# A block chain on Trainium2: the operands of the delta rule prepared without Pool, with r by channel tiles in front and the key products between the steps of the first inverse

## The reference, cut to what matters

```
kk = k * k_k;  kk = kk / max(|kk|, 1e-12)          # per head
k  = k * (1 + (a - 1) * k_a)
for t in tokens:                                    # state S is 64x64 per head
    S = S * w_t + (S @ (-kk_t)) (kk_t * a_t)^T + v_t k_t^T
    y_t = S @ r_t
y = group_norm(y) * lnx_g + lnx_b + sum(r * k * r_k) * v
out = x + gate * ([y * silu(g_r), y_a * silu(g_a)] @ w_out)
```

## Time and profile before

| | |
|---|---|
| median of 3 runs | 1930.52 us (1925.89 to 1934.94) |
| profiled execution | 1928.67 us, span 1926.8 us |
| TensorE busy | 1851.0 us, 96% of the span |
| VectorE busy | 1028.7 us, 53% |
| ScalarE busy | 648.9 us, 34% |
| Pool busy | 172.2 us, 9% |
| granted TensorE clock, mean | 0.983 |
| stretch of the second block's projections and delta rule | about 1430 to 1790 us |

### The profile page before, as it was taken

How to read it: one execution, slowest core, us unless ns; L and a number is a source line. 1 busy time by engine, 2 the same in 40 slices (tenths; PEclk the granted TensorE clock), 3 DMA queues, 4 the chain that set the end, 5 groups by cost and what they waited for, 6 DMA issues and landing times.

```text
span 1926.8 us, 27348 instructions
## 1 busy us (share of the span) xinstructions
PE 1851.0 (96%) x11475; PEld 1529.8 (79%) x11475; DVE 1028.7 (53%) x1440; ACT 648.9 (34%) x999; POOL 172.2 (9%) x190
## 2 busy tenths in 40 slices
PE   7999999999999999999999999999989899998978
PEld 7879868888888898889868888878867787776546
DVE  4467347444454564446336556654566655445653
ACT  4332442323334322232432332334346232333441
POOL 3101001000000010001001000000020211111330
PEclk9999999999999999999999999999999999999998
DMA  8323323333323324332333545423232211114111
GB/s 269 113 88 109 99 66 99 120 93 94 98 88 121 98 90 119 98 110 99 99 105 122 155 149 164 143 88 99 77 109 61 59 57 35 46 35 143 41 37 44
DMA packets 145257, 189.65 MB, mean 98 GB/s; under 512 B 7688, under 2 KB 94980, under 8 KB 144240
## 3 DMA queue, kind: packets, MB, share of 16 engines
q1 hardware_dynamic: 139088, 168.32, 28.0%
q0 software_dynamic: 3488, 10.07, 1.6%
q10 hardware_dynamic: 2560, 9.53, 1.3%
HBM read 181.58 MB, written 6.30 MB: 98 GB/s over the span
## 4 chain that ended last, share of the span: by engine, by line
PE 87%; DVE 6%; issue 2%; ACT 2%; DMA 1%; POOL 1%; POOLq 0%; ACTq 0%; DVEq 0%
PE ps L324 25%; PE ps L325 24%; PE ps L326 24%; PE ps L2039 2%; PE ps L932 1%; PE ps L908 1%; PE ps L2025 1%; DVE WL L308 1%; PE ps L1472 1%; PE ps L2000 1%; ACT WH L298 1%; DMA RAW<-ab_w_in 1%; PE ps L509 1%; PE ps L2160 1%; PE ps L1493 1%
## 5 line engine op out<-in xcount | busy, mean ns | idle before, releaser
L308 DVE TENSOR_TENSOR WL<-RAW,WH 128x1024 fp32r<-128x1024 f32 x289 | 356.6, 1247 | 526.2 <-ACT WH L298 525.5
L324 PE MATMUL ps<-XH,WH 128*128 128x512 f32 (+1 forms) x1416 | 525.5, 371 | 3.9 <-DVE XL L522 3.5
L326 PE MATMUL ps<-XH,WL 128*128 128x512 f32 (+1 forms) x1416 | 519.2, 367 | 0.0
L325 PE MATMUL ps<-XL,WH 128*128 128x512 f32 (+1 forms) x1416 | 519.2, 367 | 0.0
L298 ACT ACTIVATE WH<-RAW 128x1024 fp32r<-128x1024 f32 x289 | 301.6, 1057 | 609.8 <-PE ps L326 577.9
L324 PE MATMUL ps<-WH,XH 128*128 128x512 f32 x800 | 322.4, 403 | 11.8 <-issue 4.2
L325 PE MATMUL ps<-WL,XH 128*128 128x512 f32 x800 | 315.4, 394 | 0.0
L326 PE MATMUL ps<-WH,XL 128*128 128x512 f32 x800 | 314.9, 394 | 0.0
L324 PEld LDWEIGHTS ps<-XH,WH 128*128 128x128 f32 x1416 | 268.8, 190 | 55.5 <-issue 9.3
L326 PEld LDWEIGHTS ps<-XH,WL 128*128 128x128 f32 x1416 | 268.5, 190 | 43.8
L325 PEld LDWEIGHTS ps<-XL,WH 128*128 128x128 f32 x1416 | 268.9, 190 | 41.5 <-issue 0.5
(11 more groups left out here) (332 smaller groups left out, 1960.3 us busy)
## 6 DMA issues: line engine op xcount, KB each, us to landing
RAW<-ffn_w_up SPq DMA_DIRECT2D x176, 256.0 KB, 3.2
RAW<-ffn_w_down SPq DMA_DIRECT2D x44, 512.0 KB, 3.6
RAW<-w_in SPq DMA_DIRECT2D x33, 512.0 KB, 3.9
RAW<-xa_wkv SPq DMA_DIRECT2D x32, 512.0 KB, 4.0
RAW<-c_w_in SPq DMA_DIRECT2D x24, 512.0 KB, 3.7
LATE<-w_ada SPq DMA_DIRECT2D x24, 512.0 KB, 4.9
RAW<-xa_wq SPq DMA_DIRECT2D x16, 512.0 KB, 5.5
RAW<-xa_wo SPq DMA_DIRECT2D x16, 512.0 KB, 3.7
```

The lines of the kernel that those rows point to most:

```text
L308: e.tensor_tensor(wl[:, :, 0:w], raw(i)[:, :, 0:w], wh[:, :, 0:w].bitcast(F), ALU.subtract).then_inc(*w_lo.up(i))
L324: e.matmul(o, lh, rh, start=start, stop=False)
L325: e.matmul(o, lh, rl, start=False, stop=False)
L326: return e.matmul(o, ll, rh, start=False, stop=stop)
```

## The change

The preparation has ten turns in place of eleven, and Pool has no part in it any more. On VectorE b and a fall on one turn. r is made by channel tiles (`r_dve`): tiles 0 to 2 at turn 7, tile 3 at turn 9, with k, formerly Pool's, at turn 8 between them. kt, rk and the `rkb` columns move to `tail_dve`, steps 3, 5 and 7 of the first inverse; rk moves from Pool to VectorE. Waits follow: the products with kt wait for kt, the others for r.

```diff
--- before.py
+++ after.py
@@ -1401,8 +1401,7 @@
                 elif i:
                     e.wait_ge(*at_pe.at(("qk", 0, 3)))
                 else:
-                    e.wait_ge(*pr_v.at("r"))
-                    e.wait_ge(*pr_g.at("rk"))
+                    e.wait_ge(*pr_v.at("rk"))
                 e.wait_ge(*p2_a.at(("qkv", i, n)))
                 e.activation(sq[i][n % 2], QK[i][0][n], ACT.Square).then_inc(*at_a.up(("sq", i, n)))
             if n == 4:
@@ -1803,7 +1802,7 @@
             e.matmul(b[:, :], selT[:, 128 * m:128 * m + 128], rs8, start=True, stop=True).then_inc(*pr_pe.up(("norm", m)))
             ps.back(("norm", m))
         yield
-        for n in range(6):
+        for n in range(5):
             yield
 
     def prep_act(e):
@@ -1837,7 +1836,7 @@
         yield
         e.wait_ge(*pr_a.at("p"))
         e.activation(B[2], B[2], ACT.Exp, scale=-1.0).then_inc(*pr_a.up("1/p"))
-        for n in range(5):
+        for n in range(4):
             yield
 
     def prep_dve(e):
@@ -1866,7 +1865,6 @@
         e.wait_ge(*pr_a.at(("x0", 3)))
         e.wait_ge(*pr_v.at("kk"))
         e.scalar_tensor_tensor(out=B[1], in0=B[1], scalar=1.0, in1=L[3], op0=ALU.add, op1=ALU.mult).then_inc(*pr_v.up("b"))
-        yield
         e.wait_ge(*pr_a.at("p1"))
         e.wait_ge(*spx.at("x"))
         e.scalar_tensor_tensor(out=ar[:, :, 0, :], in0=L[3].rearrange(by_col, j=64), scalar=-1.0,
@@ -1876,33 +1874,23 @@
         e.wait_ge(*pr_v.at("b"))
         e.scalar_tensor_tensor(out=B[1], in0=B[1], scalar=0.5, in1=B[2], op0=ALU.mult, op1=ALU.mult).then_inc(*pr_v.up("bt"))
         yield
-        e.wait_ge(*pr_g.at("k"))
-        e.wait_ge(*pr_v.at("bt"))
-        e.tensor_tensor(B[2], B[5], B[2], ALU.mult).then_inc(*pr_v.up("kt"))
-        yield
-        for m in range(4):
-            e.tensor_scalar(rkb[:, m, :], bones, vec("rk", m), None, ALU.mult).then_inc(*pr_v.up(("rkb", m)))
-        yield
-        e.tensor_copy(pC, B[3].rearrange("p (a c k) -> p a c k", a=4, k=64)[:, :, :, 63]).then_inc(*pr_v.up())
-        e.wait_ge(*p2_v.at(("r", 3)))
-        e.tensor_tensor(ar[:, :, 1, :], B[4].rearrange(by_col, j=64), B[3].rearrange(by_col, j=64),
-                        ALU.mult).then_inc(*pr_v.up("r"))
-        yield
+        for m in range(3):
+            r_dve(e, m)
+        yield
+        e.tensor_tensor(B[5], B[5], L[1], ALU.mult).then_inc(*pr_v.up("k"))
+        yield
+        r_dve(e, 3)
+        e.tensor_copy(pC, B[3].rearrange("p (a c k) -> p a c k", a=4, k=64)[:, :, :, 63]).then_inc(*pr_v.up("last p"))
+        yield
+
+    def r_dve(e, m):
+        e.wait_ge(*p2_v.at(("r", m)))
+        e.tensor_tensor(ar5[:, m, :, 1, :], R[:, m, :].rearrange("p (c j) -> p c j", j=64),
+                        v4(B[3])[:, m, :].rearrange("p (c j) -> p c j", j=64), ALU.mult).then_inc(*pr_v.up("r"))
 
     def prep_own(e):
-
-        for n in range(5):
-            yield
-        e.wait_ge(*pr_a.at(("x0", 3)))
-        e.wait_ge(*pr_v.at("kk"))
-        e.tensor_tensor(B[5], B[5], L[1], ALU.mult).then_inc(*pr_g.up("k"))
-        for n in range(5):
-            yield
-        e.wait_ge(*pr_v.at("kt"))
-        e.wait_ge(*p2_v.at(("r", 3)))
-        e.wait_ge(*pr_g.at("k"))
-        e.tensor_tensor(B[5], B[4], B[5], ALU.mult).then_inc(*pr_g.up("rk"))
-        yield
+        for n in range(10):
+            yield
 
     def tail_pe(e):
 
@@ -1942,7 +1929,17 @@
             yield
 
     def tail_dve(e):
+
         for n in range(11):
+            if n == 3:
+                e.wait_ge(*pr_v.at("k"))
+                e.tensor_tensor(B[2], B[5], B[2], ALU.mult).then_inc(*pr_v.up("kt"))
+            if n == 5:
+                e.wait_ge(*pr_v.at("kt"))
+                e.tensor_tensor(B[5], B[4], B[5], ALU.mult).then_inc(*pr_v.up("rk"))
+            if n == 7:
+                for m in range(4):
+                    e.tensor_scalar(rkb[:, m, :], bones, vec("rk", m), None, ALU.mult).then_inc(*pr_v.up(("rkb", m)))
             if n >= 9:
                 for m in (20 - 2 * n, 21 - 2 * n):
                     e.wait_ge(*pr_pe.at(("bonus", m)))
@@ -1994,7 +1991,7 @@
         def masked(name, src):
             for par, p in enumerate(pps):
                 b = bank(name, par)
-                e.wait_ge(*pr_v.at("r"))
+                e.wait_ge(*pr_v.at("kt" if name == "ka" else "r"))
                 for m in range(4):
                     for cp in range(2):
                         r = e.matmul(b[pps[cp], 128 * m:128 * m + 128], src[p, m, cols[cp]],
@@ -2077,7 +2074,7 @@
                 for name, dst in (("nv", NV[t]), ("y0", Y0[t]), ("bk", Bk[t % 2]), ("kk", Kk[t % 2])):
                     e.wait_ge(*iv_pe.at((name, t)))
                     if name == "bk":
-                        e.wait_ge(*(st_pe.at(("y", 2 * t - 3)) if t >= 2 else pr_v.at("r")))
+                        e.wait_ge(*(st_pe.at(("y", 2 * t - 3)) if t >= 2 else pr_v.at("last p")))
                     if name == "nv" and t >= 2:
                         e.wait_ge(*spb.at("b"))
                     e.activation(dst, ps.tile((name, t))[:, :], ACT.Copy).then_inc(*ps.empties((name, t), iv_a, (name, t)))
```

## The result

The changed kernel takes 1935.86 us (median of 20 runs, 1931.91 to 1939.25) against 1932.23 us (20 runs, 1925.66 to 1936.79) of the kernel before beside it: a ratio of 1.0023, 95% interval 1.0014 to 1.0032. It is 0.23% slower, some 4 us, where 2.6 us of gain were forecast. Its profiled execution took 1935.91 us.

The account below looks back on a forecast made before the run. TensorE, busy 96% of the span, was taken as the bound. Terms -7.9 - 4.3 + 5.9 + 4.0 + 1.0 - 1.3 = -2.6 us gave 1926.1 from the profiled 1928.67, plus 1.85 to the median: 1927.9 us, range 1918 to 1936.

Parts of the forecast that it names:

- Term 1: Front, before the first inverse's first step: r ready earlier, so TensorE's 5.96 us wait and its half clock go, -7.9 us.
- The work moved behind the first step: kt, rk and the four small products on VectorE at steps 3, 5, 7 of the first inverse: 0 us (bounds 0 and 2).
- terms 2 to 5: Waits for the bank of w at turns 48, 38, 50 and 60, in that order: -4.3, +5.9, +4.0 and +1.0 us.
- Term 6: Turn 68, last transposes: their 4.2 us wait shortens as their chain starts a turn earlier, -1.3 us (bounds 0 and 4).
- term 2: Turn 48, u of chunk 4: the 3.23 us wait falls to 1.4 and its 2.5 us half clock goes, -4.3 us.
- Rival E: Clock stays down after close waits at turns 36 and 38: +6.9, 1937.4 us, or 1947 if repeated behind turn 50; chance 0.04.
- Rivals A: New waits at turns 38 and 50 don't come: -13.5, 1917.0 us; chance 0.14.
- B: The new waits come but no half clock follows: 5 us better, 1922.9 us; chance 0.14.
- C: At the front, r is as late as before because VectorE is held elsewhere: +5.3, 1935.8 us; chance 0.04.
- D: TensorE's queue is fixed, and equal waits behind take back what the front frees: 0, 1930.5 us; chance 0.09.

Follow-up runs that it names:

- chunk 4 or 3 early: Changed kernel, VectorE adding w's y part directly behind the state part for one chunk only: chunk 4 1930.24 us (0.9990), chunk 3 1930.42 us (0.9982), ratios against before.
- the idle turn: Changed kernel with one idle turn put back at the end of preparation (eleven turns), later steps at their old turns: 1924.34 us, ratio 0.9951 against before.

## Why the prediction was wrong, step by step

- **Term 1 (front, -7.9) held.** r was complete 1.4 us ahead of TensorE (forecast 1.1), b took 2.3, and the change with eleven turns is 9.4 us faster than before. With its interval (6.6 to 12.4) that can't be told from 7.9; the front wait was 7.5 us and not 5.96 in two of three executions of before. Cutting r cost 0.3 us: three quarters took 1.89 us and the fourth 0.69, a whole one 2.28.
- **The work moved behind the first step (0) held**: no wait of 1 us or more came between step 0 and turn 36, and the kernel with eleven turns, which has all of it, lost nothing.
- **The waits of terms 2 to 5 held to 0.2 us**: 1.35, 3.36, 3.88 and 1.18 against 1.4, 3.4, 3.9 and 1.0, with L308 right ahead of L2210 on VectorE at the 3.36 and the 3.88. Term 6 was 1.9 us and not 1.3.
- **What failed is the price of the clock, in terms 2 to 6.** For terms 2 to 4 the prediction said "the half clock after the wait costs 2.5", took it from one place, and drew a line between two rows: "I take it to go too, since a wait of 2.39 us was followed by full clock (1.00) and the one of 3.23 by 0.50". Terms 5 and 6 had no clock at all. In sum the clock was to cost 0.6 us more than before; it cost 7.0 more over all runs, and 9.7 in the three profiled executions. By stretches, in the means of these three: 4.3 less at the front (1500 to 1600 us; forecast 1.9 less), 4.3 more around turns 36 and 38 (forecast 2.5), 3.3 more around turns 48 and 50 (forecast 0), 5.6 more at turns 60 to 68 (forecast 0). The wait of 1.35 us of term 2, priced without any, was followed by a clock of 0.57 over 8 us, which is 3.4 us, in all three executions. That of 3.88 us was followed by 0.53 over 10 us, 4.7 us and not 2.5. At turns 60 to 68 it was 0.89 over 80 us against 0.96 before, in all three executions of each. The 2.5 itself was low for the place that it was read from: in the 12 us behind the wait of 3.23 us before, the clock was 0.72 in the first execution (3.4 us withheld) and 0.57 in the two others (5.2).
- **Rival E had the right direction at the wrong price.** It asked for 12 us of work at half clock in one piece. What came were several stretches, none over some 10 us in the change, behind short waits. The chance of 0.04 was too low for a cost that the argument could only bound: the two ends of the clock's price were one row each of a single execution, and neither was kept for the range.
- **The base.** The forecast stood on one profiled execution with 33 us withheld; its two repetitions have 39. So it started some 3 us below the mean of the three. It added 1.85 us for the median; the median of 20 runs, 1932.23 us, is 1.7 above the 1930.52 that it stood on.
- **Rivals A, B, C and D** are refuted: the waits came, with half clock behind them, r was early, and the later waits did not take the front's gain back by themselves: they return only 2.2 us of it.

What stays open: why the same wait of the same kernel is followed by full clock in one execution and by 10 us at half clock in another. The kernels with chunk 4 or 3 early suggest that it depends on the half clock shortly before, by one execution each; they don't show how. Also not tried was whether the waits of 1.32 and 2.27 us for the norm's last product (L2278) can be taken away in the same manner.

## What to carry to other kernels

When a turn is taken out of a schedule in which engines walk in step, list every bank that is released late on a busy engine before the time is counted: here the release of the bank of w stood a step late, at two of the waits behind a product that waits for another engine, and moving it one step forward was worth more (1.3%) than the change itself. Where TensorE is the bound, a short wait must be priced with a range for the clock behind it, here from nothing to 5 us for waits of 1.35 to 3.9 us, taken from several executions. Split each run's time by its span and mean granted clock: it tells the part of the waits (3.5 us less here) from the part of the clock (7.0 more). A gain at one place is best tested with everything behind it held in its place, as the idle turn did.

## What the hardware showed unexpectedly

A wait of 1.35 us between small matmuls was followed by half clock (0.57 over 8 us) in every execution of the change, and with that wait gone the clock there was 1.00. A pause of 3.27 us was followed by 0.86 or by 0.59 over 12 us in executions of one kernel, and by 1.00 in another that doesn't differ there. The mean granted clock of the kernel before gave 33 to 39 us withheld in three executions whose waits of 1 us or more, behind the front wait and up to 1870 us, are equal to 0.05 us; the difference is more than the effect that this case is about.
